# Moving three steps in the lead of a sublayer of a two-layer diffusion backbone on one core: VectorE's split, a split on POOL, and the mean and spread of the second half

## The reference

```python
def sandwich_in(h, m, sub, p):
    return rms_norm(h, p['norm_pre'][sub]) * (1 + m[:, 3 * sub + 1]) + m[:, 3 * sub]

def sandwich_out(h, y, m, sub, p, weight):
    return h + weight * m[:, 3 * sub + 2] * rms_norm(y, p['norm_post'][sub])

def ffn_sub(h, m, sub, j, p):
    y = swiglu(sandwich_in(h, m, sub, p), p['w_gate'][j], p['w_up'][j], p['w_down'][j])
    return sandwich_out(h, y, m, sub, p, 0.5)
```

## Time and profile before

| what | value |
|---|---|
| median of 3 runs | 3235.28 us (3230.02 to 3237.88) |
| the profiled execution | 3231.9 us, span 3230.0 us |
| PE busy | 3019.5 us, 93% of the span |
| DVE busy | 1703.0 us, 53% |
| ACT busy | 1018.8 us, 32% |
| POOL busy | 252.6 us, 8% |
| mean granted clock of TensorE | 0.966 of full speed |
| share of PE in the chain that ended last | 83% |

### The profile page before, as it was taken

How to read it: one execution, slowest core, us unless ns; L and a number is a source line. 1 busy time by engine, 2 the same in 40 slices (tenths; PEclk the granted TensorE clock), 3 DMA queues, 4 the chain that set the end, 5 groups by cost and what they waited for, 6 DMA issues and landing times.

```text
span 3230.0 us, 49425 instructions
## 1 busy us (share of the span) xinstructions
PE 3019.5 (93%) x18100; PEld 2839.0 (88%) x18100; DVE 1703.0 (53%) x3018; ACT 1018.8 (32%) x1720; POOL 252.6 (8%) x210
## 2 busy tenths in 40 slices
PE   6999999989898789999999999999988898899998
PEld 5999999969674789999999999999978765899997
DVE  4565665655246663465326575545555347643334
ACT  3212112433434442121224312112433434532233
POOL 1000000410000050000005000000320000400002
PEclk8999999999998899999999899999999998999999
DMA  6444344422100132334324344334322200423333
GB/s 204 128 127 130 110 124 130 111 69 59 56 1 1 33 98 64 98 109 122 83 62 117 107 120 129 98 90 138 104 82 59 62 1 1 125 81 102 91 92 111
DMA packets 454132, 293.21 MB, mean 91 GB/s; under 512 B 25974, under 2 KB 411356, under 8 KB 453980
## 3 DMA queue, kind: packets, MB, share of 16 engines
q1 hardware_dynamic: 453456, 291.01, 31.1%
q10 hardware_dynamic: 524, 0.18, 0.0%
HBM read 289.04 MB, written 2.10 MB: 90 GB/s over the span
## 4 chain that ended last, share of the span: by engine, by line
PE 83%; DVE 6%; POOL 4%; ACT 3%; issue 3%; DMA 1%; DVEq 0%; POOLq 0%; ACTq 0%; SPq 0%
PE ps L1683 24%; PE ps L1684 24%; PE ps L1685 24%; POOL scr L720 3%; PE ps L2082 2%; PE ps L2034 1%; PE ps L2009 1%; PE ps L2010 1%; ACT wsp L782 1%; PE ps L2067 1%; POOL wsp L729 1%; DVE wsp L1162 1%; DVE hn L1250 1%; PE ps L2021 1%; PE ps L1745 1%
## 5 line engine op out<-in xcount | busy, mean ns | idle before, releaser
L1683 PE MATMUL ps<-hn,wsp 128*128 128x384 f32 (+1 forms) x3200 | 1055.7, 330 | 48.7 <-DVE hn L1250 28.9
L1684 PE MATMUL ps<-hn,wsp 128*128 128x384 f32 (+1 forms) x3200 | 1046.5, 327 | 0.0
L1685 PE MATMUL ps<-hn,wsp 128*128 128x384 f32 (+1 forms) x3200 | 1046.5, 327 | 0.0
L1162 DVE TENSOR_TENSOR wsp<-raw,wsp 128x1024 fp32r<-128x1024 f32 x375 | 462.5, 1234 | 509.4 <-ACT wsp L782 509.4
L1683 PEld LDWEIGHTS ps<-hn,wsp 128*128 128x128 f32 x3200 | 613.3, 192 | 63.4 <-issue 33.2
L1684 PEld LDWEIGHTS ps<-hn,wsp 128*128 128x128 f32 x3200 | 613.8, 192 | 0.0
L1685 PEld LDWEIGHTS ps<-hn,wsp 128*128 128x128 f32 x3200 | 613.2, 192 | 0.0
L782 ACT ACTIVATE wsp<-raw 128x1024 fp32r<-128x1024 f32 x408 | 429.1, 1052 | 532.9 <-PE ps L1685 532.8
L1683 PE MATMUL ps<-aT,wsp 128*128 128x384 f32 (+1 forms) x1408 | 459.5, 326 | 23.3 <-DVE aT L1341 19.3
L1684 PE MATMUL ps<-aT,wsp 128*128 128x384 f32 (+1 forms) x1408 | 455.3, 323 | 0.0
L1685 PE MATMUL ps<-aT,wsp 128*128 128x384 f32 (+1 forms) x1408 | 455.1, 323 | 0.0
(11 more groups left out here) (209 smaller groups left out, 2957.0 us busy)
## 6 DMA issues: line engine op xcount, KB each, us to landing
modw<-in_w_mod SPq DMA_DIRECT2D x144, 512.0 KB, 4.2
raw<-in_ffn_w_gate SPq DMA_DIRECT2D x192, 256.0 KB, 3.4
raw<-in_ffn_w_up SPq DMA_DIRECT2D x192, 256.0 KB, 4.1
raw<-in_ffn_w_down SPq DMA_DIRECT2D x64, 448.0 KB, 3.4
raw<-in_w_in SPq DMA_DIRECT2D x96, 256.0 KB, 3.0
raw<-in_ffn_w_down SPq DMA_DIRECT2D x64, 256.0 KB, 4.1
raw<-in_w_out SPq DMA_DIRECT2D x64, 256.0 KB, 3.2
raw<-in_ffn_w_down SPq DMA_DIRECT2D x64, 192.0 KB, 3.5
```

The source lines that it names most:

```text
L1162: dve.tensor_tensor(wsp[:, cs, 1, 0:width], raw[:, slot, 0:width], wsp[:, cs, 0, 0:width].bitcast(F32), ALU.subtract).then_inc(wlo_done, 1)
L1683: pe.matmul(dst, w(0), x(0), start=first, stop=False)
L1684: pe.matmul(dst, w(0), x(1), start=False, stop=False)
L1685: return pe.matmul(dst, w(1), x(0), start=False, stop=last)
```

## The change

It edits the table `LEAD`, one line of `split_by_pool` and the place of the hook.

```diff
             i = t - CONV - first_tile0(l, sub)
             if 0 <= i < HEAD:
-                return i == 0 and (l, sub) != (0, 0)
+                return i in (0, 3) and (l, sub) != (0, 0)
...
 LEAD = {
-    "DVE": [("mean", 1, 1), ("post", 1, 0), ("post", 1, 2), ("head", 1), ("post", 1, 4), ("post", 1, 6), ("head", 2),
-            ("mean", 0, 1), ("pre", 1, 0), ("pre", 1, 2), ("head", 3), ("pre", 1, 4), ("pre", 1, 6)],
-    "ACT": [("mean", 1, 1), ("head", 0), ("xsq", 1, 0), ("head", 1), ("xsq", 1, 2), ("xsq", 1, 4), ("head", 2),
-            ("xsq", 1, 6), ("mean", 0, 1), ("head", 3)] + [("pre", 1, k) for k in PAIRS],
-    "POOL": [("head", 0)] + [("xsq", 1, k) for k in PAIRS],
-    "PE": {(0, 5): ("mean", 1, 1), (0, 7): ("spread", 1, 1), (3, 4): ("mean", 0, 1), (3, 7): ("spread", 0, 1)},
+    "DVE": [("mean", 1, 1), ("post", 1, 0), ("post", 1, 2), ("post", 1, 4), ("head", 1), ("post", 1, 6), ("head", 2),
+            ("mean", 0, 1)] + [("pre", 1, k) for k in PAIRS],
+    "ACT": [("mean", 1, 1), ("head", 0), ("xsq", 1, 0), ("xsq", 1, 2), ("head", 1), ("xsq", 1, 4), ("xsq", 1, 6),
+            ("head", 2), ("mean", 0, 1), ("head", 3)] + [("pre", 1, k) for k in PAIRS],
+    "POOL": [("head", 0)] + [("xsq", 1, k) for k in PAIRS] + [("head", 3)],
+    "PE": {(0, 5): ("mean", 1, 1), (0, 6): ("spread", 1, 1), (3, 6): ("mean", 0, 1), (3, 8): ("spread", 0, 1)},
 }
...
                 ins.then_inc(unit_done, 1)
+                if ready is not None:
+                    ready(G)
```

More of the change, by code:

```diff
@@ L1769, in last_pass @@
                         last_output(l, sub, 0, dt, dt, None if dt else
-                                    lambda k: pe.wait_ge(mlo_done, 16 * l + k + 1))
+                                    lambda k: k < KD and pe.wait_ge(mlo_done, 16 * l + k + 1))
                     pe.wait_ge(mlo_done, 16 * (l + 1))
@@ L1786, in input_ready @@
             def input_ready(l, sub, n):
-                return lambda k: pe.wait_ge(hlo_done, KD * pre_event(l, sub, n) + k + 1)
+                return lambda k: k < KD and pe.wait_ge(hlo_done, KD * pre_event(l, sub, n) + k + 1)
             def small_steps(hooks, i, prev, cur, ready=None):
                 def hook(k):
-                    if ready is not None:
+                    if ready is not None and k < KD:
                         ready(k)
```

## The result

| | before | after |
|---|---|---|
| median of 6 runs each | 3232.65 us (3226.78 to 3237.88) | 3214.38 us (3212.62 to 3217.60) |
| ratio, with its 95% interval | | 0.9948 (0.9937 to 0.9959) |
| span of the profiled execution | 3230.0 us | 3210.7 us |

The kernel became faster by 0.52%, 17 us by the ratio and 18.3 us between the two medians. The forecast was 3216.5 us, a gain of 18.6. Further runs of the kernel before, taken beside the change, brought its median from 3235.28 to 3232.65.

What follows compares the result with a forecast made beforehand. TensorE, busy 93% of the span, bounds the kernel, so only its waits and slow stretches can be saved. Four leads at 4.5 us plus 2.4, less 1.8 for the clock, gave 18.6 us: 3216.5 us, range 3206 to 3229.

Steps and rivals of the forecast that it cites:

- Spread of y one chunk earlier: In each lead, TensorE waits 0.70 us for the reciprocal; alone the edit costs up to 0.52 us a lead.
- Reordering: Tile 3's splits moved later: POOL's 1.19 us wait goes, additions bind and end at 655.5, not 656.05; 0.5 us gained.
- Mean at (3, 6), spread at (3, 8): Wait ahead of the mean 1.9 us, not 3.80; VectorE's `pre` starts 2.5 us earlier, including the reordering's 0.5.
- the clock behind it: Low clock between mean and `pre` costs 1.3 us; given a third of the leads, 1.8 us off the sum.
- Tile 5's split on POOL: Tile 5 starts 10.05 us behind `pre`, not 12.07: 2.0 us a lead; POOL's split of 2.4 us stays hidden.
- The fifth lead: The lead with halves of 256 tokens: 2.4 us shorter, and the mean does not come earlier.
- The sum: Four leads of 4.5 us and 2.4 in the fifth: 20.4, less 1.8 for the clock, 18.6 us.
- The rule on shared ports: VectorE's two splits beside POOL's additions: 1.43 us stretch kept; an exclusive lock would make the sum 5 us less.
- POOL's split holding VectorE up: Rival: POOL's new split beside `pre` stops VectorE 2.4 us in every lead; 12 us given back, 3228 us; chance 0.05.
- A gain given back later: Rival: something behind the lead is fixed in time, half or more of 18.6 goes, 3226 or above; chance 0.07.
- The slower case: Rival: low clock stays behind every lead through tiles 4 to 6; 19 us slower, 3255 us; chance 0.04.
- the full clock: Rival: with the mean's wait halved, all five leads run as the first; gain 25 us, 3210 us; chance 0.12.

Runs made afterwards that it cites:

- its undoing: The changed kernel with the spread of y back at (0, 7): median 3211.13 us, 0.9942 of before.
- the run of POOL's split alone: The kernel before with only the split of tile 5 moved from VectorE to POOL: median 3226.70 us, 0.9982 of before.
- Products that only hold the clock: Unread identity products in TensorE's waits, in four kernels: spread at (0, 7) 0.9937, tile 2 split by VectorE 0.9913, before 0.9989, before with tile 3's splits reordered 0.9957.
- the run with the reordering alone: The kernel before with only VectorE's and ScalarE's splits of tile 3 moved later: median 3236.39 us, 1.001 of before.
- the run without the reordering: The changed kernel with spread of y at (0, 7) and tile 3's splits in their old places: median 3216.56 us, 0.9951 of before.
- the run with the mean at (3, 7): The changed kernel with spread of y at (0, 7), tile 2 split by VectorE and mean of x at (3, 7): median 3195.07 us, 0.9901 of before.
- late mean and spread alone: The kernel before with only mean and spread of x moved to (3, 6) and (3, 8): median 3222.41 us, 0.9981 of before.
- the reordered kernel with products: The kernel before with tile 3's splits reordered and unread identity products in TensorE's waits: median 3215.41 us, 0.9957 of before.

## Why the prediction was right, point by point

- **Spread of y one chunk earlier**: right. The wait is 0.55, not 0.70, and the edit alone costs 0.5 us a lead on the mean, as put; shown by its undoing.
- **Reordering**: right in kind, a little off in size. POOL's wait among the additions went and the additions bind; they end 0.35 us earlier than before, not 0.5, because the two splits beside them stretched them by 1.6 us and not 1.4 (9.57 for seven that would take 7.98).
- **Mean at (3, 6), spread at (3, 8)**: the wait came out at 1.88 us against 1.9. (The two are not counted alike. The profile counts from the end of the last product; so counted, the forecast has 1.75, and the mean came 0.14 us later than put.) The step that was mis-sized is the clock behind it. It was given a third of the leads; it was low between mean and `pre` wholly or in part in three of the four wide leads: `pre` starts 3.8, 3.7 and 4.3 us behind the mean there, 2.7 (the forecast) only in the fourth. So 1.2 was gained at the start of `pre` in the first lead, not 2.5.
- **Tile 5's split on POOL**: right. Tile 5 starts 10.06 us behind `pre` in the first lead (forecast 10.05), 10.1 in the second and 10.4 and 10.5 in the third and fourth; POOL's split took 2.35 us with 7 us to spare.
- **The fifth lead**: 2.23 us, forecast 2.4.
- **The sum**: 20.4 before the clock and 18.6 with it, 19.9 measured in the windows. That it fits so well is partly luck: the first two leads gained 1.2 and 1.1 less than put, and the fourth 2.2 more, since the low clock that held before through its tiles 4 and 5 ended earlier. Both are the clock, and the run of POOL's split alone shows that the third and fourth lead can lose their low clock without a shorter wait ahead of the mean.
- **The rule on shared ports**: the Trainium skill ("SBUF — State Buffer", SBUF: two separate sides and Who interferes with whom) has the port that VectorE and POOL share as an exclusive lock: whichever instruction starts first, of VectorE's with two SBUF inputs and POOL's that reads SBUF, holds it to its end. The prediction put the price of this at 1.23 us on the additions for each split, 2.5 in all, and kept the 1.43 of the rows; the run shows 1.6. The single instructions of the first lead, before and after (the lines shown merge them), agree with the lock even so. Each of the four additions that started during a split had 0.84 to 0.95 us of the split still before it, and took 0.69 to 0.80 us more than the 1.02 us it takes alone. The three splits that started during an addition, with 0.37, 0.47 and 0.84 us of it left, took 0.23, 0.32 and 0.69 more than 1.23. In each of these seven cases the later one lost what was left of the earlier less about 0.15 us. So a split does not cost its whole length, but what of it the next addition meets. The part of the rule that VectorE with one SBUF input does not contend is borne out by POOL's 2.35 us beside `pre`.
- **The rivals**: POOL's split holding VectorE up is refuted by the run of that edit alone. A gain given back later did not happen in this kernel, but it did in others, and by the clock, which the prediction had only within the leads. The slower case did not come, nor did the full clock: the leads ran at 0.83 to 0.90.

## What to carry to other kernels

Where an engine's chain is waited for by name, read what stands ahead of it in that engine's own order: the change left POOL's 2.4 us ahead of its additions in place, and moving them shortened the leads by 6.5 us more. A step of under 5 us in a kernel whose TensorE often changes its clock is told by the trace and not by the time: stretches that nobody touched, with low clock in them, moved the total by 7 to 9 us in four of the runs, up or down. Windows are of one execution and hold low clock too (4 us in the run of POOL's split alone), so the surest reading is the distance of a step from the first mean, which came out within 0.1 us in all four wide leads wherever no low clock stood between. Products that only hold the clock did what they should where they stood, and the total gained less than that, or lost.

## What the runs showed of the hardware that was not expected

A wait of 1.88 us ahead of the mean was followed by the low level of the clock (0.96 us a chunk, 1.2 GHz) in three of four leads, and one of 1.03 us was not. In the run with the reordering alone the wait was shorter than before (2.90 against 3.80 us) and the granted clock in the lead lower (0.83 against 0.91): a shorter wait is no promise of a higher clock. Nor does the length of the wait alone decide. In the run without the reordering the same wait was followed by low clock in the first lead and by full clock in the fourth:

```profile
656.57 0.97 PE L1698 MATMUL ps<-cst,scr 128*128 128x1 f32 x6 [2.80 <-POOL scr L720]
657.39 0.67 PE L1683 MATMUL ps<-hn,wsp 128*128 128x384 f32 x1
657.86 0.52 PE L1684 MATMUL ps<-hn,wsp 128*128 128x384 f32 x1
```
```profile
2361.54 0.80 PE L1698 MATMUL ps<-cst,scr 128*128 128x1 f32 x6 [2.79 <-POOL scr L720]
2362.20 0.42 PE L1683 MATMUL ps<-hn,wsp 128*128 128x384 f32 x1
2362.46 0.34 PE L1684 MATMUL ps<-hn,wsp 128*128 128x384 f32 x1
```

The Trainium skill ("TensorE: Matmul & The Clock Gate", The two states you'll see) has the low state behind idleness; the traces agree with it, 0.52 us a chunk before a wait and 0.96 behind.

The stretch of the first mixer, with 2282 or 2283 recorded products in all runs, took 495.5 us (the run with the mean at (3, 7), granted clock 0.95) to 502.8 us (late mean and spread alone, 0.92), and that of the second 411.5 us (0.95) to 419.7 us (the reordering alone, 0.92). The changes ahead of the mixers cannot be the whole cause, since executions of one and the same program differ as much: those of the reordered kernel with products took 3208.53 us at a mean granted clock of 0.980 to 3220.88 us at 0.971. What makes an execution fall into the one or the other stays open: no run varied the moment at which a mixer begins alone.
